# A hybrid attention and expert block on one core: 64-byte steps between weight slots, and 64 key tiles in 256-column products

## The reference, cut to what matters

```
h = jnp.einsum('thkd,td->thk', u_tab[e], xc)
act = jax.nn.gelu(h, approximate=False) * gate
return jnp.einsum('thk,thkd->td', act, v_tab[e])
```

## Time and profile before

| | us |
|---|---|
| median of 3 runs | 1012.79 (1012.19 to 1013.17) |
| the profiled execution's own time | 1012.39 |
| its span, first to last instruction | 1010.6 |

### The profile page before, as it was taken

How to read it: one execution, slowest core, us unless ns; L and a number is a source line. 1 busy time by engine, 2 the same in 40 slices (tenths; PEclk the granted TensorE clock), 3 DMA queues, 4 the chain that set the end, 5 groups by cost and what they waited for, 6 DMA issues and landing times.

```text
span 1010.6 us, 21094 instructions
## 1 busy us (share of the span) xinstructions
PE 1006.0 (100%) x7310; PEld 898.7 (89%) x7310; DVE 794.4 (79%) x1368; ACT 526.2 (52%) x853; POOL 460.8 (46%) x198
## 2 busy tenths in 40 slices
PE   9999999999999999999999999999999999999998
PEld 9999999999999999988888888788888888888886
DVE  6999785867999993288888888988888867676764
ACT  6654877644545445545555555544444444444443
POOL 4654456756699999943444433100000004444442
DMA  6684446655455566545554455555555555655562
GB/s 240 225 290 157 132 147 201 200 183 167 149 187 193 181 205 201 192 153 170 175 172 166 166 166 168 192 184 176 174 166 166 170 183 173 201 176 197 177 198 83
DMA packets 52618, 181.93 MB, mean 180 GB/s; under 512 B 5943, under 2 KB 9155, under 8 KB 52452
## 3 DMA queue, kind: packets, MB, share of 16 engines
q1 hardware_dynamic: 52292, 181.16, 54.2%
q10 hardware_dynamic: 288, 0.27, 0.1%
HBM read 180.33 MB, written 3.43 MB: 182 GB/s over the span
## 4 chain that ended last, share of the span: by engine, by line
PE 97%; ACT 1%; DVE 1%; issue 0%; POOL 0%; DVEq 0%; ACTq 0%; POOLq 0%
PE bank L1564 35%; PE bank L1242 33%; PE bank L1499 12%; PE bank L1501 6%; PE bank L1513 3%; PE bank L1343 2%; PE bank L1257 1%; PE bank L1475 1%; PE bank L1590 1%; PE bank L1266 1%; ACT hi L335 1%; PE bank L1359 1%; PE bank L1382 0%; DVE lo L354 0%; PE bank L1370 0%
## 5 line engine op out<-in xcount | busy, mean ns | idle before, releaser
L354 POOL TENSOR_TENSOR lo<-raw,hi 128x1024 fp32r<-128x1024 f32 x184 | 457.9, 2503 | 535.3 <-ACT hi L335 535.0
L335 ACT CAST hi<-raw 128x1024 fp32r<-128x1024 f32 x332 | 347.3, 1047 | 224.0 <-PE bank L1564 193.5
L1564 PE MATMUL bank<-hi,norm_space 128*128 128x512 f32 x1008 | 280.3, 397 | 0.0
L1242 PE MATMUL bank<-norm_space,hi 128*128 128x256 f32 x1600 | 276.4, 278 | 0.2 <-POOL lo L354 0.2
L1242 PEld LDWEIGHTS bank<-norm_space,hi 128*128 128x128 f32 x1600 | 241.6, 188 | 1.8 <-issue 1.2
L1564 PEld LDWEIGHTS bank<-hi,norm_space 128*128 128x128 f32 x1008 | 187.9, 188 | 44.6
L354 DVE TENSOR_TENSOR lo<-raw,hi 128x1024 fp32r<-128x1024 f32 x148 | 189.4, 1280 | 44.3 <-ACT hi L335 41.7
L1242 PE MATMUL bank<-norm_space,lo 128*128 128x256 f32 x800 | 221.6, 277 | 0.0
L1499 PE MATMUL bank<-norm_space,hi 128*128 128x512 f32 x512 | 182.8, 400 | 0.0
L1564 PE MATMUL bank<-lo,norm_space 128*128 128x512 f32 x504 | 158.3, 395 | 0.0
L1161 DVE TENSOR_TENSOR norm_space<-act,norm_space 128x256 fp32r<-128x256 f32 x128 | 111.2, 871 | 50.3 <-ACT norm_space L677 50.3
(11 more groups left out here) (190 smaller groups left out, 955.4 us busy)
## 6 DMA issues: line engine op xcount, KB each, us to landing
raw<-u_tiles SPq DMA_DIRECT2D x128, 512.0 KB, 3.3
raw<-v_tiles SPq DMA_DIRECT2D x128, 512.0 KB, 3.3
raw<-front SPq DMA_DIRECT2D x76, 512.0 KB, 4.0
toeplitz<-bias_row SPq DMA_DIRECT2D x6, 384.0 KB, 7.4
bias<-toeplitz SPq DMA_DIRECT2D x12, 128.0 KB, 4.0
resid<-x_t SPq DMA_DIRECT2D x2, 512.0 KB, 4.6
qk<-sub_keys SPq DMA_DIRECT2D x1, 1024.0 KB, 7.7
y<-act SPq DMA_DIRECT2D x3, 256.0 KB, 2.0
```

What stands on the lines that cost most here:

```text
L335: act_e.copy(hi[:, s, :], raw[:, s, :]).then_inc(hi_ready, 1)
L354: eng.tensor_tensor(lo[:, s, :], raw[:, s, :], hi[:, s, :].bitcast(F32), ALU.subtract)\
L1242: ins = pe.matmul(dst, w_[:, s, u * P:(u + 1) * P], x_[:, k, :], start=first and i == 0 and p_ == 0, stop=last and i == n - 1 and p_ == 2)
L1564: ins = pe.matmul(bank[2 * c + half][:, :], a_[:, j, c * P:(c + 1) * P], v_[:, j, half * 512:(half + 1) * 512], start=False, stop=False, s ...
```

## The change

`SLOT_STEP` = 16 floats (64 bytes) follow each slot of `hi` and `lo`, `RAW_PAD` = 0 the ring `raw`, and `PART_PAD` = 64 floats the whole of `hi`. The activations' parts begin `ACT_SHIFT` = 24 floats into `norm_space` instead of 0. `half_sum` is no longer there, and so everything behind it lies 2048 bytes lower: `raw` begins at 176352, `hi` at 192736, `lo` at 209632. The last 64 key tiles use `u_tile` in place of `wide_tile`; ScalarE's GELU reads the bank, and the copy, the addition and their semaphores are gone. In a round ScalarE now rounds the weights before it applies the GELU, and in the last round the wait for `blocks_free` stands between the two.

```diff
+SLOT_STEP, RAW_PAD, PART_PAD = 16, 0, 64
+ACT_SHIFT = 24
-        picked_acts = norm_space[:, 0:RING * 2 * T].rearrange("p (k a t) -> p k a t", a=2, t=T)
+        picked_acts = norm_space[:, ACT_SHIFT:ACT_SHIFT + RING * 2 * T].rearrange("p (k a t) -> p k a t", a=2, t=T)
...
-        half_sum = sb("half_sum", [P, 2, T])
-        raw = sb("raw", [P, RING, D])
-        hi = sb("hi", [P, RING, D], F32R)
-        lo = sb("lo", [P, RING, D], F32R)
+        raw_space = sb("raw_space", [P, RING * D + RAW_PAD])
+        raw = raw_space[:, 0:RING * D].rearrange("p (r d) -> p r d", r=RING)
+        hi_space = sb("hi_space", [P, RING * (D + SLOT_STEP) + PART_PAD], F32R)
+        lo_space = sb("lo_space", [P, RING * (D + SLOT_STEP)], F32R)
+        hi, lo = [x[:, 0:RING * (D + SLOT_STEP)].rearrange("p (r d) -> p r d", r=RING)[:, :, 0:D]
+                  for x in (hi_space, lo_space)]
...
-            def key_round(it, first=False, last=False):
+            def key_round(it, last=False):
                 for j in range(RING):
+                    split_hi(a, U0 + HALF + LEAD, it, j)
                     if last and j == RING - 1:
                         a.wait_ge(gated, GROUPS_N)
                         a.wait_ge(blocks_free, 1)
                         for first_act in range(AHEAD):
                             a_split(first_act, 0, 0)
-                    copy_cross(it, j)
-                    if not (first and j == 0):
-                        gelu_sum(-1, it, j)
-                    split_hi(a, U0 + HALF + LEAD, it, j)
+                    gelu(HALF, it, j)
...
-                        add_halves(it, j)
...
-            def u_tile(base_i, it, j):
+            def u_tile(base_i, it, j, last=False):
 
                 wait(pe, gelu_done, it * 4 + (base_i + j - 1))
-                ins = product(bank[4 + j % 2][:, 0:T], j, [(k, k) for k in range(KB)], nrm_hi, nrm_lo, U0 + base_i, it, j)
+                b, units = bank[4 + j % 2][:, 0:T], [(k, k) for k in range(KB)]
+                if last:
+                    product(b, j, units[:RING], nrm_hi, nrm_lo, U0 + base_i, it, j, last=False).then_inc(blocks_free, 1)
+                    ins = product(b, j, units[RING:], nrm_hi, nrm_lo, U0 + base_i, it, j, first=False)
+                else:
+                    ins = product(b, j, units, nrm_hi, nrm_lo, U0 + base_i, it, j)
...
-                    wide_tile(it, j, last and j == RING - 1)
+                    u_tile(HALF, it, j, last and j == RING - 1)
```

More of the change, by code:

```diff
@@ L292, in hybrid_block @@
         sc_ready = sem("sc_ready")
-        crossed, added, gelu_done = sem("crossed"), sem("added"), sem("gelu_done")
+        gelu_done = sem("gelu_done")
         top_done, gexp, gate_ready, pick_T, pick_ready = [sem(s) for s in (
@@ L661, in _ @@
             a.wait_ge(pick_ready, 2)
[L662 to L672, removed]
             def a_split(base_i, it, j):
@@ L685, in key_round @@
                             a_split(first_act, 0, 0)
-                    copy_cross(it, j)
-                    if not (first and j == 0):
-                        gelu_sum(-1, it, j)
-                    split_hi(a, U0 + HALF + LEAD, it, j)
-            key_round(0, first=True)
-            with a.Fori(1, HALF // RING - 1) as it:
+                    gelu(HALF, it, j)
+            with a.Fori(0, HALF // RING - 1) as it:
                 key_round(it)
             key_round(HALF // RING - 1, last=True)
-            gelu_sum(HALF - 1, 0, 0)
             a.wait_ge(pe_step, S_V)
@@ L1162, in low_part @@
                                   ALU.subtract).then_inc(a_lo, 1)
[L1164 to L1168, removed]
             def gate_body(half, it, first=False, last=False):
@@ L1189, in gate_body @@
                         one_hots(1, 0, j - 1)
[L1190 to L1193, removed]
-                        add_halves(it, j)
+                    if half == 0 and last and j == RING - 1:
+                        for first_act in range(AHEAD):
+                            low_part(first_act, 0, 0)
                     if by_dve(base + LEAD, j):
@@ L1481, in _ @@
                     freed(pe, job)
-            def u_tile(base_i, it, j):
+            def u_tile(base_i, it, j, last=False):
                 wait(pe, gelu_done, it * 4 + (base_i + j - 1))
-                ins = product(bank[4 + j % 2][:, 0:T], j, [(k, k) for k in range(KB)], nrm_hi, nrm_lo, U0 + base_i, it, j)
[L1487 to L1493, removed]
-                else:
[L1495 to L1504, removed]
+                b, units = bank[4 + j % 2][:, 0:T], [(k, k) for k in range(KB)]
+                if last:
+                    product(b, j, units[:RING], nrm_hi, nrm_lo, U0 + base_i, it, j, last=False).then_inc(blocks_free, 1)
+                    ins = product(b, j, units[RING:], nrm_hi, nrm_lo, U0 + base_i, it, j, first=False)
+                else:
+                    ins = product(b, j, units, nrm_hi, nrm_lo, U0 + base_i, it, j)
                 ins.then_inc(pe_step, 1)
```

## The result

The changed kernel takes 1019.11 us (median of 3 runs, 1018.92 to 1019.98), the one before 1012.79: a ratio of 1.0067, 95% interval 1.0047 to 1.0087. It is slower, by 0.7%. The forecast was 1005.9 us, faster, with a range up to 1015.

What follows compares the result with a forecast made beforehand. TensorE's matmul count and spacing were taken as the bound. From the profiled 1012.4 us, Part 1 took 6.5 and Part 2 counted 0, giving 1005.9 us; its own range was 1003.5 to 1008.5, the 8-in-10 range 995 to 1015.

Steps and rivals of the forecast that it cites:

- What bounds the kernel: Whole kernel: only TensorE's matmul count and spacing matter; it is busy 1006.0 of 1010.6 us and waits 1.4 us.
- Two pitches for 256 columns: Front and keys: 256-column matmuls start either 113.4 or 117.8 ns apart, a difference of 4.4 ns each.
- the front: Stages before the keys, query projection included: new places give -3.0 us at best, +2.2 if the 504 tight matmuls turn loose.
- Part 1: Last key half: 24 products of 256 columns per tile save 6.5 us, provided they run at the tight pitch.
- tight: The shorter spacing of 256-column matmuls, 113.4 ns, seen in 1440 matmuls of the first key half.
- Part 2: New operand places in front, keys and values: taken as 0, with ends of -18.7 and +12.4 us.
- the loose pitch: The longer spacing of 256-column matmuls, 117.8 ns, seen in 312 matmuls of the query projection.
- Rival 4: First key half: new distances throw TensorE out of the tight pitch, +6.8 us, last half gains 0; 1019.2 us, chance 0.17.
- Rival 1: Values and front: the new distances shorten the stream too, by 5.1 and 3.0 us; 997.8 us, chance 0.25.
- Rival 2: Last key half: the narrow tiles run at the loose pitch, so nothing is gained; 1012.4 us, chance 0.09.
- Rival 3: Last key half: each extra matmul start costs 2.2 ns, 1.1 us in all; 1013.5 us, chance 0.02.
- The pitch has survived every slot change so far: Argument about the first key half, set against Rival 4's 1019.2 us: earlier slot changes left the matmul spacing unchanged.

Runs made afterwards that it cites:

- parts 1 and 2 alone: Two kernels, each the kernel before with one part: only the 256-column products, 1007.13 us; only the new operand places, 1017.17 us; both against 1012.49.
- part 1 alone: The kernel before with 24 products of 256 columns per tile in the last key half, old operand places kept: 1007.13 us against 1012.49, ratio 0.9942.

## Why the prediction was wrong

**What bounds the kernel: right.** TensorE alone, without waits, before and after.

**Two pitches for 256 columns: right, and too narrow.** They are the two of one distance, 64 bytes. I read the pieces of the front and of the keys and all their slots as samples of one thing, but they all lay at that distance, so the rows could not show what another does.

**Part 1, -6.5 us if tight: right where its premise holds.** Alone it measured -5.4 us by the medians and -6.1 from the keys' start to the values'; the round is 11.96 us against the forecast 11.94. With the new places the premise doesn't hold: slots 1 to 3 don't come out tight, the round is 12.36, and the last key half takes 0.2 us more than before.

**Part 2, taken as 0 between -18.7 and +12.4: the step that failed.** Its sentence was "I take 0: within the rows of before, the distance hardly shows". The two rows it rests on (values at -96 bytes 116.7, wide keys at +64 bytes 117.6 per 256 columns) stream 512 columns in one case and 512 and 256 in turn in the other, so they don't compare two distances. The table shows that -96 is one of the values' poor distances, and parts 1 and 2 alone show that wide and narrow products answer to the distance differently (a wide round gained 0.11 us by the new places, a narrow one lost 0.40). Measured by stretch: front +3.7 (I had bounded its tight piece by +2.2, and it was +2.4), first key half +6.4 of a bound of +6.8, part 1 undone, values -3.6. The first key half and the values came out within their bounds, the front beyond. The bounds took the loose pitch, 117.8 ns, for the worst, where a tile at 256 bytes has 120.3. For a loss of this size I had 0.17.

**Rivals.** Rival 4 is what happened: a step of 64 bytes throws the stream out of the tight pitch in the first key half, and the last one gives nothing; its 1019.2 us is the measured time, though by luck in the sum, as the front's 3.7 and the values' -3.6 cancel. In one thing its cause was off, as far as the runs tell: not the change of distance does it, but the distance. Rival 1 was right for the values, where the 96 bytes were named as the odd one: they gain, by 3.6 us for the mixed distances and 9.4 for the best one tried. But that 96 is no multiple of 64 isn't the reason: -128 and -192 are multiples and cost 2795 ns a tile, 16 is none and costs 2728. Rival 2, the narrow tiles loose behind the gates, fell with part 1 alone. Rival 3, the fixed price of a start, didn't show: part 1 alone would have been slower. "The pitch has survived every slot change so far" counted against rival 4 what spoke neither way, since no slot change before had changed the distance.

The Trainium skill ("SBUF — State Buffer", "Who interferes with whom") has TensorE wait for nobody and read both operands through ports of their own. The runs don't agree: with nothing but the activations' place changed, a value tile takes 2720 ns in place of 2800. They don't show what in the reading or loading of the two operands is late.

## What to carry to other kernels

Where TensorE is the bound and loads fresh weights for each matmul, the distance between loaded and streamed operand is a parameter like any other: read the starts of single matmuls by tile, keep every slot of a ring at one distance (modulo 256 bytes here), and scan that distance for each form of product. A scan of four distances fits into one run, by a step between the slots, but read it as a first look: neighbours carried 20 to 38 ns a tile over here, so the best one is then tried in all slots. As a final layout such a step gives the mean of four prices. And where all rows of a profile lie at one value of a quantity, they don't say that the quantity doesn't matter.

## What the runs showed of the hardware that I had not expected

- fp32r matmuls of 256 columns with a new 128 x 128 load each start 113.3 ns apart at a distance of 64 bytes (modulo 256) in all slots, and 117.7 to 120.3 at the others tried, each in a ring of mixed distances; of 512 columns 226.7 ns at distance 0 in all slots, 227.3 at 16, 229.8 at -64 and 232.9 to 234.6 at the others. The best distance is not the same for the two.
- At 64 bytes the 256-column stream has two lasting pitches, 113.3 and 117.8 ns. What stands ahead of a stretch can change which: moving 16 transposes behind the query projection turned 288 of its matmuls tight. Why one interruption is followed by this pitch and another by that is open, as is the mechanism behind the distance; no experiment looked into either further.
- The tight pitches, 113.3 and 226.7 ns, are 272 and 544 periods of the granted 2.4 GHz, 16 more than the columns and 32 more. It is an observation, not explained here.
